# Scatters of a long convolution: issued by SyncE instead of GpSimd

## The reference

```python
def bidir_long_conv(z, h_fwd, h_bwd, bias):
    L = z.shape[1]
    k = jnp.concatenate([h_fwd, jnp.zeros_like(h_fwd[:1]), h_bwd[1:][::-1]], axis=0)
    kf = jnp.fft.rfft(k.astype(jnp.float32), n=2 * L, axis=0)
    zf = jnp.fft.rfft(z.astype(jnp.float32), n=2 * L, axis=1)
    y = jnp.fft.irfft(zf * kf, n=2 * L, axis=1)[:, :L]
    return (y + z.astype(jnp.float32) * bias).astype(z.dtype)

    z = v                                   # in hyena_mixer
    for n, gate in enumerate((x1, x2)):
        z = gate * bidir_long_conv(z, filt[:, n, 0], filt[:, n, 1], fbias[n])
```

## Time and profile before

| | |
|---|---|
| time, three runs | 3744.97, 3747.05, 3752.88 us, median 3747.05 |
| profiled execution | 3743.57 us, of which the span of the trace is 3741.8 |
| convolution stage in the trace | from about 428 to 1142 us |
| TensorE busy | 90% of the span, mean granted clock 0.953 |
| GpSimd's DMA queue | 131.27 MB, 16.5% of the 16 engines' span |
| SP's DMA queue | 270.68 MB, 22.3% |

### The profile page before, as it was taken

The page is one execution under the profiler, slowest core; times in us unless marked ns, Lnnn a source line. Parts: engine busy times, 40 slices in busy tenths (PEclk is TensorE's granted clock), DMA queues, the critical chain, the costliest instruction groups (busy, mean ns, idle before and its releaser), DMA issues.

```text
span 3741.8 us, 47892 instructions
## 1 busy us (share of the span) xinstructions
PE 3368.0 (90%) x18246; PEld 2622.9 (70%) x18246; DVE 2181.8 (58%) x3240; ACT 1316.5 (35%) x2215; POOL 314.1 (8%) x510
## 2 busy tenths in 40 slices
PE   3999867887888899999999988999999979999897
PEld 2888534454467778888778866767777758888685
DVE  8998723333334665555476855555555676666676
ACT  2221222332333443333234643333333353333344
POOL 0111123333330000000000110000000000000000
PEclk9999989888888999999999999999999989999999
DMA  6665879878653132222443531000000223332632
GB/s 220 217 202 197 188 105 140 118 115 135 130 172 110 57 124 84 83 83 81 180 152 96 166 113 40 8 7 7 14 24 0 78 102 110 108 104 87 239 99 87
DMA packets 184985, 410.13 MB, mean 110 GB/s; under 512 B 33279, under 2 KB 60223, under 8 KB 183111
## 3 DMA queue, kind: packets, MB, share of 16 engines
q1 hardware_dynamic: 132584, 270.68, 22.3%
q0 software_dynamic: 51936, 131.27, 16.5%
q10 hardware_dynamic: 288, 5.77, 0.4%
HBM read 262.50 MB, written 81.00 MB: 92 GB/s over the span
## 4 chain that ended last, share of the span: by engine, by line
PE 71%; DVE 12%; DMA 11%; ACT 3%; issue 3%; POOL 1%; SPq 0%; DVEq 0%; ACTq 0%
PE ps L618 18%; PE ps L620 18%; PE ps L619 18%; DMA t2w<-w 4%; PE ps L2367 3%; PE ps L2392 3%; DMA t2z<-s 2%; DMA t2k<-s 2%; PE ps L688 1%; PE ps L2240 1%; DVE mx L2758 1%; PE ps L2264 1%; PE ps L2249 1%; PE ps L2427 1%; PE ps L2330 1%
## 5 line engine op out<-in xcount | busy, mean ns | idle before, releaser
L618 PE MATMUL ps<-HB,gsp 128*128 128x512 f32 x1232 | 488.6, 397 | 37.2 <-DVE HB L794 21.9
L619 PE MATMUL ps<-HB,gsp 128*128 128x512 f32 x1232 | 485.2, 394 | 0.0
L620 PE MATMUL ps<-HB,gsp 128*128 128x512 f32 x1232 | 484.1, 393 | 0.0
L1072 DVE TENSOR_TENSOR gsp<-graw,gsp 128x512 fp32r<-128x512 f32 x330 | 226.4, 690 | 262.7 <-ACT gsp L1051 261.9
L1051 ACT ACTIVATE gsp<-graw 128x512 fp32r<-128x512 f32 x330 | 206.7, 628 | 326.9 <-PE ps L620 265.0
L618 PEld LDWEIGHTS ps<-HB,gsp 128*128 128x128 f32 x1232 | 234.5, 190 | 90.1 <-issue 21.4
L618 PE MATMUL ps<-tsp,wdh 128*128 128x512 f32 x616 | 244.1, 396 | 35.3 <-DVE tsp L1329 35.2
L620 PEld LDWEIGHTS ps<-HB,gsp 128*128 128x128 f32 x1232 | 234.3, 190 | 49.8
L619 PEld LDWEIGHTS ps<-HB,gsp 128*128 128x128 f32 x1232 | 234.6, 190 | 46.8 <-issue 1.0
L619 PE MATMUL ps<-tsp,wdh 128*128 128x512 f32 x616 | 242.4, 394 | 0.0
L620 PE MATMUL ps<-tsp,wdh 128*128 128x512 f32 x616 | 242.3, 393 | 0.0
(11 more groups left out here) (263 smaller groups left out, 7717.2 us busy)
## 6 DMA issues: line engine op xcount, KB each, us to landing
graw<-in_w_gu SPq DMA_DIRECT2D x176, 256.0 KB, 2.6
mring<-in_mod_w POOLq DMA_DIRECT2D x78, 512.0 KB, 4.7
hidden_scratch<-R SPq DMA_DIRECT2D x154, 256.0 KB, 2.4
traw<-hidden_scratch SPq DMA_DIRECT2D x154, 256.0 KB, 2.6
t2k<-s POOLq DMA_DIRECT2D x80, 256.0 KB, 10.1
t2z<-s POOLq DMA_DIRECT2D x160, 128.0 KB, 8.8
t2w<-w POOLq DMA_DIRECT2D x160, 128.0 KB, 5.1
wd<-in_w_dx SPq DMA_DIRECT2D x6, 2816.0 KB, 14.2
```

Of the source, the lines that this page charges most:

```text
L618: pe.matmul(o, wh, xh, start=start, stop=False, skip_group_check=onto)
L619: pe.matmul(o, wh, xl, start=False, stop=False, skip_group_check=onto)
L620: return pe.matmul(o, wl, xh, start=False, stop=stop, skip_group_check=onto)
L1072: dve.tensor_tensor(gsp[U % 3][:, 1, :], graw[:, q, W_SLOT[i], :], gsp[U % 3][:, 0, :].bitcast(F32), ALU.subtract).then_inc(w.lo, 1)
```

## The change

SP's walk now issues the scatters of K, Z and M, with the same waits and the same semaphores that GpSimd had. GpSimd's walk is gone; in its place GpSimd loads `mi` and `mib` once the input projection is done. In SP's list some other steps move with it: the filter inputs are loaded ahead of the last scatter of a K step, the first gate of a round goes out between the scatters of units 3 and 4 of M instead of ahead of M, and the first three weight tiles of the output projection go out between units 1 and 2 of the last M instead of after the walk. Sizes, buffers and semaphore counts stay.

```diff
-            sp.wait_ge(p_in.full, 24 * 6)
-            sp.dma_start(mi[:], a["k_mi"][:, 0]).then_inc(s_ci, 16)
-            sp.dma_start(mib[:], a["k_mi"][:, 1]).then_inc(s_ci, 16)
             for kind, it, o, n in WALK:
                 if kind == "K":
+                    for u in range(8):
+                        if it == NCH and o == 0 and u in (5, 7):
+                            filter_load(NCH + 2 + u // 7)
+                        if it < NCH and o == 1 and u == 7:
+                            filter_load(it + 2)
+                        n2, cc, kb = filter_unit(it, o, u)
+                        b = n["B"] + u
+                        sp.wait_ge(s_be, b + 1)
+                        sp.dma_start(by_partition(t2k, it, n2, 0 if it < NCH else 512 * cc, 512), s1[b % 6][:]
+                                     ).then_inc(s_s1o[b % 6], 16)
                 elif kind == "Z":
+                    for u in range(4):
+                        for h in range(2):
+                            b = n["B"] + 2 * u + h
+                            sp.wait_ge(s_be, b + 1)
+                            for m2 in range(2):
+                                n2, at = (2 * u + m2 + 8 * h, 0) if it < NCH else (m2 + 2 * h, CW * u)
+                                sp.dma_start(by_partition(t2z, it, n2, at, CW), s1[b % 6][:, CW * m2:CW * (m2 + 1)]
+                                             ).then_inc(s_s1o[b % 6], 16)
...
-                elif kind == "M" and o == 0:
...
+                elif kind == "M":
+                    for u in range(8):
+                        if o == 0 and u == 4:
+                            if it == 0:
+                                sp.wait_ge(s_ms, 16)
+                            else:
+                                sp.wait_ge(s_zs, 16 * it)
+                            sp.dma_start(share(gbuf, it), u_share(it, 0)).then_inc(s_gl, 16)
+                        if it == NCH and o == 1 and u == 2:
+                            sent(sp, B_END["Z", NCH, 1])
+                            for t in range(3):
+                                mix_load(sp, 0, t)
+                        d = n["d"] + u
+                        sp.wait_ge(s_de, d + 1)
+                        for h in range(2):
+                            g, at = signal_part(it, 4 * (u // 2) + 2 * h + u % 2)
+                            sp.dma_start(by_partition(t2w, it, g, CW * at, CW), w1[d % 3][:, CW * h:CW * (h + 1)]
+                                         ).then_inc(s_w1o[d % 3], 16)
...
-            sent(sp, B_END["Z", NCH, 1])
-            for t in range(3):
-                mix_load(sp, 0, t)
...
-            for kind, it, o, n in WALK:
-                if kind == "K":
...
+            pool.wait_ge(p_in.full, 24 * 6)
+            pool.dma_start(mi[:], a["k_mi"][:, 0]).then_inc(s_ci, 16)
+            pool.dma_start(mib[:], a["k_mi"][:, 1]).then_inc(s_ci, 16)
```

More of the change, by code:

```diff
@@ L1847, in _ @@
             sp.wait_ge(s_us[1], 12 * 32)
-            sp.wait_ge(p_in.full, 24 * 6)
-            sp.dma_start(mi[:], a["k_mi"][:, 0]).then_inc(s_ci, 16)
-            sp.dma_start(mib[:], a["k_mi"][:, 1]).then_inc(s_ci, 16)
             for kind, it, o, n in WALK:
                 if kind == "K":
[L1854 to L1858, removed]
-                elif kind == "Z":
+                    for u in range(8):
[8 more added lines that the diff above has]
+                                     ).then_inc(s_s1o[b % 6], 16)
+                elif kind == "Z":
+                    for u in range(4):
[6 more added lines that the diff above has]
+                                             ).then_inc(s_s1o[b % 6], 16)
                     if o == 1 and it + 1 < NIT:
```

## The result

The changed kernel takes 3820.07 us (median, 3810.69 to 3823.12) where the kernel before took 3746.01 beside it: a ratio of 1.019, 95% interval 1.0167 to 1.0214. It is slower by 71 us by the ratio and 74 by the medians. The prediction was 3793.

What follows compares the result with a forecast made beforehand. Scatters of rounds 0 to 3 queuing for the few partitions they write bound the stage. -4 + 41 + 14 - 5 = +46 us on 3743.6 gives 3790, median 3793; forecast range 3755 to 3900, over the cases 3715 to 4115.

Steps and rivals of the forecast that it cites:

- A: Rival: half of the engines carry half of the rate, 62 GB/s; +365 us, 4115; chance 0.25.
- B: Rival: flights get shorter, SP's queue starts sooner and keeps the rates; -41 us, 3706; chance 0.20.
- C: Rival: same engines and partitions set the rate whoever issues; only loads, end and issues remain; +5 us, 3752; chance 0.10.
- Issue, -4: Scatter issues on SP take 0.12 us less than on GpSimd, some 30 places on the chain: -4 us (0 to -20).
- Rate of K, +26: K steps of rounds 0 to 3 fall from 124 to 104 GB/s on half of the engines: +3.3 us, eight times.
- Z, +15: Z steps without the load of `zbuf` fall from 127 to 104 GB/s: +3.7 us, four times.
- the load of `zbuf` in line, +14: The load of `zbuf` stands in front of scatters on SP's queue: +3.5 us, four times, +14 (0 to +20).
- a stretch of over 300 GB/s in which none moves: Sign: a K step behind the load of `zbuf` shows full share, over 300 GB/s, and no scatter moving.
- M unchanged: M steps of rounds 0 to 3 keep 104 GB/s and 20.2 us on SP's queue: no change.
- The gate inside M, 0 (-8 to +12): The first gate's load interrupts M's scatters at unit 4; same bytes, same step: 0 us (-8 to +12).
- `mi` and `mib`, 0: Constants on GpSimd's queue still go out when the input projection ends, covered by first K and Z steps: 0 us.
- The end, -5: At the stage's end the last scatters land ahead of the loads of x, so B starts earlier: -5 us (0 to -11).

Runs made afterwards that it cites:

- m_on_sp: Changed kernel with only M's scatters on SP, those of K and Z left on GpSimd as before: 3780.26 us, ratio 1.0102 to the kernel before.
- the spread order: Units of K and M in rounds 0 to 3 taken as 0, 4, 1, 5, 2, 6, 3, 7: 3771.92 us with scatters on SP, 3664.82 on GpSimd.
- loads_pool2: Changed kernel with the loads of `zbuf` and of the first gate issued by GpSimd at the same places: 3806.55 us, ratio 1.0174.
- order_only: Kernel before, scatters on GpSimd, with only the first gate moved after M's unit 3 and `mi`, `mib` on GpSimd's queue: 3754.44 us, ratio 1.0052.
- gate_first: Changed kernel with a round's first gate loaded ahead of M's first scatter again: 3798.06 us, ratio 1.0151 to the kernel before.
- spread_sp: Changed kernel with units of K and M in rounds 0 to 3 taken as 0, 4, 1, 5, 2, 6, 3, 7: 3771.92 us, ratio 1.0067.
- spread_gate_sp: Changed kernel with units ordered 0, 4, 1, 5, 2, 6, 3, 7 and the first gate at M's unit 0: 3751.54 us, ratio 1.0025.
- end_pool: Kernel before with SP's seven loads of x at the stage's end held until the last scatters land: 3739.18 us, ratio 0.9998.
- step4_sp: Changed kernel, scatters of rounds 0 to 3 to partitions 4 apart instead of 16, convolution not right, time only: 3632.39 us, ratio 0.9688.
- step4: Scatters of rounds 0 to 3 to partitions 4 apart, time only: 3632.39 us on the changed kernel, 3632.74 on the kernel before.

## Why the prediction was right, and where its terms were off

The mechanism and the sign held: half of the engines on SP's queue (share 0.47 to 0.57), 104 GB/s forecast and 95 to 106 found where scatters are queued (124 in Z(.,0)), 3793 forecast and 3820 measured, inside the forecast's own range of 3755 to 3900. That the sum came as near is luck in part: its terms for K, Z and `zbuf` were 22 us too large, and those for M and the gate, which it put at nothing, 38 too small. Of the rivals, A's 62 GB/s is in no window (95 is the lowest of K), B's gain needs scatters that overlap on SP's queue as on GpSimd's, and C is refuted by the share. The terms one by one:

- **Issue, -4.** Wrong: 0. A scatter's issue takes 597 ns on SP, at the upper of the two bounds. The value in the middle had no row behind it; loads with fewer pieces to describe were the nearest rows, and they were not near enough. The chain even has longer issues of SP, behind scatters that have not landed (SPq L1889, 2.28 us).
- **Rate of K, +26, and Z, +15, and the load of `zbuf` in line, +14; together +55.** After less m_on_sp gives 33 us (20 to 46) for the three. The rate was right in K; what a lower rate costs was not. The sum multiplied bytes by rate and took each step as bound by its flights from end to end. In the chain of before K(.,1) is on no link of the round shown: that step had slack, and the first microseconds were hidden. And Z(.,0), the step to which the +15 belonged, kept 124 GB/s on half of the engines. Why, wasn't tried; its scatters are of 128 KB and change between rows 8 apart, as the spread order does for M. The +14 for `zbuf` took the load as a block in front of the scatters, with a stretch of over 300 GB/s in which none moves; that sign did not come (135 to 248 GB/s at 9 tenths). Both loads out of the line, in loads_pool2, gave 6 us by the ratios and 14 by the medians, not clear of nothing.
- **M unchanged.** Wrong: +19 (m_on_sp less order_only). M's rate of 101 to 106 at a share of 0.75 is a mean over flight and pause. I read it as a rate that half of the engines can hold, while its flights themselves got longer, from 4.6 to 5.3 us to 6.1 to 6.5 (gate_first), and ACT's wait for `w` grew from 110.5 us in order_only to 126.8 in m_on_sp. A mean rate below the full share says nothing of how fast a flight is.
- **The gate inside M, 0 (-8 to +12).** Wrong, above its bound: +16 to +19 (order_only; spread_sp less spread_gate_sp). "Same bytes, same step" forgot the three buffers `w1`. Ahead of M a part of the gate's load overlaps the matmuls before the first scatter (the first flight is 9.26 us before); at unit 4 ACT is already waiting for buffers, and the flight of 10.79 us stops it, and PE behind it, once a round.
- **`mi` and `mib`, 0.** They are part of order_only and can't be told from the gate there; no wait of PE for them is in the chain. Nothing speaks against it.
- **The end, -5.** Right in its mechanism, but nearly worth nothing. Last scatters that don't queue behind the loads of x give B at the full clock, in after as in end_pool (7.11 us). The weights of the output projection then are what is late next, which the prediction did not ask. The ratio of end_pool bounds it at -4.5 to +3.4.

By the ratios the parts are: order with gate 19, M 19, K, Z and `zbuf` 33. They are steps from before over order_only and m_on_sp to after, so they add up to 71 by construction, and each is good to 12 or 13 us (the first to 6). The prediction's sum of +46 had its errors on both sides: 22 too much in K, Z and `zbuf`, 38 too little in M and the gate, 9 too much gain in issue and end.

Two of its readings were loose. The row of 190 GB/s at a share of 0.53 for round 4 holds the filter inputs too (0.77 of 2.46 MB); the better sign of fast scatters there is that 256 KB land in 3.4 us, beside 10.0 in rounds 0 to 3. And in the rivals' prices A's 4115 is 3 us above the 3747 + 365 that its text gives, and the range over the cases begins at 3715, above B's own 3706.

What the prediction did see and did not follow: that "in rounds 0 to 3 the scatters queue for the few partitions that they write". The gain lay there. The order in which the units write, with the scatters left on GpSimd, is worth 76 to 86 us.

## What to carry to other kernels

A rate below the full DMA share is a mean over flight and pause; cost a slower queue by the length of the flights on the chain and by the buffers that wait for them, not by bytes over the mean. A load ahead of a step can hide a part of itself behind the matmuls that come before the first buffer is needed; in the middle it can't: look at how many buffers are free where it starts. And where the engines are full but slow, look at which partitions successive transfers write before looking at who issues them: alternating the two halves of the units gave 2.3% (2.0% by the medians), moving the issue cost 1.9%.

## What the runs showed of the hardware

- A scatter to 8 partitions, issued by SP, keeps about half of the 16 DMA engines busy, however many are queued (slices of 3 to 6 tenths in K, 0.47 to 0.57 over the windows of after without a load; 0.48 and 0.53 in step4_sp). A scatter to 32 partitions on the same queue reaches 9 tenths. Issued by GpSimd, two in a row use both halves (1.04). The Trainium skill's rule on how many engines a DMA uses ("DMA: Bandwidth & Descriptors", section "Why a DMA increments its semaphore by 16 and not by 1") fits this; the numbers of the engines were not seen.
- The rate into 8 partitions depends on which they are: on SP's half of the engines 95 to 124 GB/s at 16 apart and 177 at 4 apart; on GpSimd a K step fills the engines (1.04) for 124 GB/s at 16 apart and moves 136 at a share of 0.57 at 4 apart. The kernels differ in nothing else.
- Scatters and a load in one queue of SP move side by side: 9 tenths of the engines for some 6 us at 135 to 248 GB/s, and the load of 1 MB lands after 18.1 us.
- SP's issue of a DMA, 0.60 us in the median, lasts up to 5.9 us where many scatters have not landed, and everything behind it in SP's list waits.
- Half of the engines lost only a sixth of the rate (124 to 103). That 16 engines were too many for these partitions fits this and step4, but was not tried by itself. The spread order is worth 46 us on SP, where the rate in K rises by 13% only; most of it shows in M's flights and ACT's waits for them.
